# Two expert layers: 64 of 256 tokens look their experts up, 192 go through all experts; plain float32 first weights, ten products a unit

## The reference, cut to what matters

```python
def block(xc):                                   # per 128 tokens
    q = (xc @ w_q).reshape(128, 8, 2, 128)
    sc = einsum('thpd,hpnd->thpn', q, subkeys)   # 2 x 128 keys a head
    s1, i1 = top_k(sc[:, :, 0], 16)
    s2, i2 = top_k(sc[:, :, 1], 16)
    cand = s1[..., :, None] + s2[..., None, :]   # 256 sums a head
    top, pos = top_k(cand, 16)
    idx = ...i1 * 128 + i2 at pos...             # [128 tokens, 128 experts]
    gate = softmax(top)
    u_e, v_e = u[idx], v[idx]                    # u, v: [16384, 1024]
    act = gelu(einsum('ted,td->te', u_e, xc))
    return einsum('te,ted->td', gate * act, v_e)
```

## Time and profile before

| | |
|---|---|
| median of three runs | 2287.76 us (2285.74 to 2288.77) |
| profiled execution, first to last instruction | 2284.1 us |
| PE busy | 2268.4 us, 99% |
| DVE busy | 1699.0 us, 74% |
| ACT busy | 1324.8 us, 58% |
| POOL busy | 430.5 us, 19% |
| moved by DMA | 408.53 MB, 179 GB/s on average |
| PE's share of the chain that ended last | 87% |

### The profile page before, as it was taken

The page is one execution under the profiler, slowest core; times in us unless marked ns, Lnnn a source line. Parts: engine busy times, 40 slices in busy tenths (PEclk is TensorE's granted clock), DMA queues, the critical chain, the costliest instruction groups (busy, mean ns, idle before and its releaser), DMA issues.

```text
span 2284.1 us, 33324 instructions
## 1 busy us (share of the span) xinstructions
PE 2268.4 (99%) x12380; PEld 1929.4 (84%) x12380; DVE 1699.0 (74%) x3098; ACT 1324.8 (58%) x2181; POOL 430.5 (19%) x355
## 2 busy tenths in 40 slices
PE   9999999999999999999999999999999999999999
PEld 9788888888888888887788888888888888877887
DVE  7567588999975555668758898997555666877885
ACT  3454555578765554646555558776555564666554
POOL 1000233178710000000013316872000000000000
PEclk9999999999999999999999999999999999999999
DMA  7455455544455655644455554445556575333555
GB/s 257 156 176 190 161 191 189 183 167 156 149 194 193 203 193 194 231 163 142 141 171 187 193 177 169 153 155 190 194 193 232 184 227 179 135 123 118 185 186 173
DMA packets 112096, 408.53 MB, mean 179 GB/s; under 512 B 12592, under 2 KB 12640, under 8 KB 111680
## 3 DMA queue, kind: packets, MB, share of 16 engines
q1 hardware_dynamic: 107712, 391.63, 50.4%
q0 software_dynamic: 3504, 13.47, 1.7%
q10 hardware_dynamic: 720, 1.31, 0.2%
HBM read 405.30 MB, written 1.05 MB: 178 GB/s over the span
## 4 chain that ended last, share of the span: by engine, by line
PE 87%; DVE 9%; ACT 2%; issue 1%; DMA 1%; POOL 0%; ACTq 0%; DVEq 0%
PE ps L716 24%; PE ps L633 21%; PE ps L705 12%; PE ps L636 11%; PE ps L672 3%; PE ps L669 3%; PE ps L676 3%; DVE lo L1967 3%; PE ps L915 2%; PE ps L768 1%; DVE big L1973 1%; ACT hi L1373 1%; DVE big L2303 1%; PE ps L889 1%; PE ps L616 1%
## 5 line engine op out<-in xcount | busy, mean ns | idle before, releaser
L1967 DVE TENSOR_TENSOR lo<-raw,hi 128x1024 fp32r<-128x1024 f32 (+1 forms) x627 | 765.4, 1224 | 366.1 <-ACT hi L1373 363.6
L1373 ACT ACTIVATE hi<-raw 128x1024 fp32r<-128x1024 f32 x677 | 714.3, 1057 | 479.7 <-PE ps L716 270.7
L633 PE MATMUL ps<-xs,hi 128*128 128x512 f32 x2560 | 650.8, 396 | 1.0 <-DVE big L2918 1.0
L633 PEld LDWEIGHTS ps<-xs,hi 128*128 128x128 f32 x2560 | 459.2, 189 | 83.6 <-DVE big L2918 1.1
L636 PEld LDWEIGHTS ps<-xs,lo 128*128 128x128 f32 x2560 | 349.0, 190 | 25.8
L636 PE MATMUL ps<-xs,lo 128*128 128x256 f32 x2560 | 356.3, 282 | 0.0
L2998 POOL TENSOR_SCALAR lnp<-iota,selT 128x128 f32<-128x128 f32 x256 | 278.1, 1097 | 167.0 <-DVE negT L2345 88.9
L705 PE MATMUL ps<-hi,lefts 128*128 128x512 f32 x986 | 304.0, 389 | 0.0
L716 PE MATMUL ps<-lo,lefts 128*128 128x512 f32 x986 | 303.7, 389 | 0.0
L716 PE MATMUL ps<-hi,lefts 128*128 128x512 f32 x986 | 303.6, 389 | 0.0
L716 PEld LDWEIGHTS ps<-hi,lefts 128*128 128x128 f32 x986 | 184.9, 188 | 38.7 <-DVE lefts L2033 0.2
(11 more groups left out here) (370 smaller groups left out, 2505.8 us busy)
## 6 DMA issues: line engine op xcount, KB each, us to landing
raw<-in_peer_u SPq DMA_DIRECT2D x256, 512.0 KB, 3.2
raw<-in_peer_v SPq DMA_DIRECT2D x256, 512.0 KB, 4.2
raw<-in_ret_vg SPq DMA_DIRECT2D x32, 512.0 KB, 3.2
raw<-in_peer_q SPq DMA_DIRECT2D x24, 512.0 KB, 3.2
raw<-in_ffn_up SPq DMA_DIRECT2D x22, 512.0 KB, 3.3
raw<-in_ffn_down SPq DMA_DIRECT2D x22, 512.0 KB, 4.0
raw<-in_ffn_gate SPq DMA_DIRECT2D x18, 512.0 KB, 4.3
raw<-in_ret_qk SPq DMA_DIRECT2D x16, 512.0 KB, 4.6
```

The costliest lines, as they stand in the source:

```text
L633: e.matmul(out, uh[:, k, :], xs[:, k, :, :].rearrange("p h t -> p (h t)"), start=k == 0, stop=False)
L1373: e.activation(parts(i)[0][:, 0:w], raw[:, i % N_RAW, 0:w], ACT.Copy).then_inc(s_hi, 1)
L1967: e.tensor_tensor(ul[:, 0:w], raw[:, i % N_RAW, 0:w], uh[:, 0:w].bitcast(F32), ALU.subtract).then_inc(s_lo, 1)
```

## The change

**64 tokens are looked up.** The first 64 tokens (of token tile 0) use gathers: for each layer, 64 gathers of u rows and 64 of v rows. Each gather brings 128 rows of 4 KB, one to a partition: partitions 0 to 63 hold one chosen expert of each token, partitions 64 to 127 another. DVE multiplies a u gather with copies of x and sums it (`look`, q < 64), and later adds a v gather times its weight to `Peer.sums`. POOL issues the gathers from its queue (`look_up`), with four row buffers.

**192 tokens stay dense.** The first weights are no longer split: `peer_u` leaves the ring of units, and SP loads it into `plain` (six places over the room of `hi` and `lo`). PE multiplies 8 slices of plain float32 weights with 192 columns of plain float32 x (`Peer.xT`). The groups of four tokens are 48 instead of 64.

**Ten products a unit.** For tile 0 of the second weights the left side is one block of 128 columns: the low parts of its 64 dense tokens in columns 0 to 63 and their high parts in 64 to 127. It is multiplied with the high and the low weights (4 products of 512 columns, `mixed`); tile 1 keeps its 6. At the end `fold` adds the two halves and the looked-up sums with four plain float32 products.

**Moved.** The top-16 steps run 15 a unit and must be done in chunk 12; PE turns the gates at c == 14 (was 34). The 50 group steps stand in c >= 17, five in every nine units (were in c >= 36, five in every four). Looks stand three in every five units from c == 9, then five in every nine units of `peer_v`. POOL's low parts move from 25 units of `peer_u` to every third of the first 99 units of `peer_v`. The diff, cut to its core:

```diff
-FREE = 84
+LOOKED = 64
+DENSE = S - LOOKED
+GROUPS = DENSE // 4
+N_PLAIN, N_ROWS = 6, 4
+YIELDS, LISTED, SPREAD, LOOKS = 15, 14, 17, 9
+LOOK_PAIRS = 64
...
+            n = 1 if c >= SPREAD and (2 * (c - SPREAD) + j) % 9 < 5 else 0
+            steps[c, j] = list(range(at, min(at + n, GROUPS + 2)))
...
+            n = 1 if c >= LOOKS and (2 * (c - LOOKS) + j) % 5 < 3 and q < LOOK_PAIRS else 0
+            looks[c, j] = list(range(q, q + n))
...
+    for k in range(128):
+        n = 1 if k >= 3 and q < 2 * LOOK_PAIRS and (k - 3) % 9 < 5 else 0
+        looks[k] = list(range(q, q + n))
...
-        POOL_UNITS = (*range(1, 27, 2), *range(35, 59, 2))
+        POOL_UNITS = tuple(range(3, 99, 3))
...
+            for r in range(N_SPLIT):
+                n = min(n for n in in_ring[r] if n >= end)
+                m = max(m for m in range(128 * l, 128 * l + 128) if m % N_PLAIN % N_SPLIT == r)
+                W.after[n] = (*W.after.get(n, ()), (s_pused, m + 1))
@@ PE, first weights @@
-                        feat_wide(n + j, u.view[:, j, :], X_PEER[l])
+                        e.wait_ge(*plain_landed(m))
+                        for k in range(8):
+                            ins = e.matmul(u.view[:, j * DENSE:(j + 1) * DENSE], w[:, k, :], Peer.xT[:, k, :],
+                                           start=k == 0, stop=k == 7)
...
-                    if c == 34:
+                    if c == LISTED:
                         for t in range(2):
                             e.wait_ge(s_gate, 2 * l + t + 1)
@@ PE, second weights @@
+                def mixed(k):
+                    (uh, ul), left = parts(n0 + k), left_parts(q0 + k)[0][:, 0:128]
+                    e.wait_ge(s_hi, n0 + k + 1)
+                    e.wait_ge(s_ll, q0 + k + 1)
+                    for i, w in enumerate((uh, ul)):
+                        if i:
+                            e.wait_ge(*low(n0 + k))
+                        for f in range(2):
+                            ins = e.matmul(us[f].view, left, w[:, f * 512:(f + 1) * 512], start=k == 0 and i == 0,
+                                           stop=k == 127 and i == 1)
...
+            def fold(l):
+                e.wait_ge(*looked(l, 2 * LOOK_PAIRS))
...
+                for f in range(2):
...
+                    e.matmul(y.view, Peer.fold[:, LOOKED:192], Peer.sums[:, cut], start=True, stop=False)
+                    e.wait_ge(*use["mixed", l, f].freed)
+                    e.matmul(y.view, Peer.fold[:, 0:128], Peer.halves[:, cut], start=False, stop=True).then_inc(y.filled[0], 1)
-            peer(0, 0, between=lambda j: xs_tile(X_DIFF, xk, normed_x(1), 0) if j == 4 else None)
+            peer(0, 0, between=lambda j: xs_tile(X_DIFF, xk, normed_x(1), 0) if j == 5 else None)
@@ DVE, left side of the second weights @@
+                    if src.shape[-1] == DENSE:
+                        e.tensor_tensor(left_h[:, 0:128 - n], src[:, 0:128 - n], left_h[:, n:128].bitcast(F32), ALU.subtract)
+                        e.tensor_tensor(left_l[:, 128:S], src[:, 128 - n:DENSE], left_h[:, 128:S].bitcast(F32),
+                                        ALU.subtract).then_inc(s_ll, 1)
@@ DVE, beside the norm: two calls @@
+                def plain_xT(t):
...
+                    for g in range(2):
...
+                        e.tensor_copy(Peer.xT[:, 4 * g:4 * g + 4, mine], v[:, :, there]).then_inc(s_xt, 1)
...
+                def look(q):
...
+                    e.wait_ge(*rows_landed(l, q))
+                    if q < LOOK_PAIRS:
+                        e.tensor_tensor_reduce(rows, rows, Peer.copies, 1.0, 0.0, ALU.mult, ALU.add,
+                                               Peer.act[:, q:q + 1]).then_inc(s_looked, 1)
+                    else:
...
+                        e.scalar_tensor_tensor(out=Peer.sums, in0=rows, scalar=w, in1=Peer.sums, op0=ALU.mult,
+                                               op1=ALU.add).then_inc(s_looked, 1)
...
-                        if c < 33 and (c, j) != (0, 0):
-                            for _ in range(5 + (j and c % 2)):
+                        if c < LISTED - 1 and (c, j) != (0, 0):
+                            for _ in range(YIELDS):
                                 next(steps, None)
...
                 def last(k):
                     if k == 0:
-                        add(63)
...
+                        gated(63)
+                    for q in LOOKS_AT[k]:
+                        look(q)
@@ POOL @@
+            def look_up(l, q):
+                table = A[f"peer_ur{l}"] if q < LOOK_PAIRS else A[f"peer_v{l}"].rearrange("n p d -> (n p) d")
+                m, i = 2 * LOOK_PAIRS * l + q, q % LOOK_PAIRS
+                if q >= N_ROWS:
+                    e.wait_ge(*looked(l, q - N_ROWS + 1))
+                e.indirect_dma_start(out=Peer.rows[m % N_ROWS], out_offset=None, in_=table,
+                                     in_offset=bass.IndirectOffsetOnAxis(ap=Peer.idx[:, i:i + 1], axis=0)
+                                     ).then_inc(s_row[m % N_ROWS], 16)
...
+                copies(l)
+                list_out(l)
...
+                for q in range(N_ROWS + 2):
+                    look_up(l, q)
+                gates_out(l)
...
+                for i in range(GROUPS):
+                    while q < GATHERS[i]:
+                        look_up(l, q)
+                        q += 1
                     build(l, i)
...
+                for k in range(128):
+                    if k in POOL_UNITS:
+                        low_part(W.first[f"peer_v{l}"] + k)
+                    for q2 in LOOKS_AT[max(0, k - 2)]:
+                        if q2 + N_ROWS < 2 * LOOK_PAIRS:
+                            look_up(l, q2 + N_ROWS)
```

More of the change, by code:

```diff
@@ L571, in build @@
                 if i >= N_SPLIT:
-                    place(W.first[stage] + k, Tail.w[i - N_SPLIT], *read(stage, 95))
+                    i -= N_SPLIT
+                    place(W.first[stage] + k, Tail.w[i], *read(stage, -(-(Tail.w_at[i] + 2 * UNIT) // DENSE)))
             for i in range(6):
-                L.own[lhs_first[stage] + 122 + i] = (*Tail.left[i], read(stage, 95))
-        place(W.first["diff_k0"] + 3, Tail.more[0], *read("peer_v0", 103))
-        for i in range(3):
-            place(W.first["diff_q0"] + i, Tail.more[1 + i], *read("peer_v0", 128))
+                L.own[lhs_first[stage] + 122 + i] = (*Tail.left[i], read(stage, 115))
+        place(W.first["diff_k0"] + 3, Tail.first[0], looked(0, 2 * LOOK_PAIRS))
+        for i in range(2):
+            place(W.first["diff_q0"] + i, Tail.first[1 + i], looked(0, 2 * LOOK_PAIRS))
+        place(W.first["diff_q0"] + 2, Tail.first[3], *read("peer_v0", 126))
         for i in range(4):
@@ L581, in build @@
             place(W.first["diff_w_out"] + 6 + i, Diff.late[i], (s_scored, 16))
-        place(W.first["w_in_c"] + 3, Tail.more[0], *read("peer_v1", 128))
+        place(W.first["w_in_c"] + 3, Tail.more[0], *read("peer_v1", 128), (s_norm, 13))
         for i in range(3):
@@ L2259, in topk @@
                                     ALU.subtract).then_inc(s_sel, 1)
+                    if t == 0:
+                        first, second = (a.rearrange("p h k -> p (h k)") for a in Peer.sel[0][0:2])
+                        e.scalar_tensor_tensor(out=Peer.listed, in0=first, scalar=128.0, in1=second, op0=ALU.mult,
+                                               op1=ALU.add).then_inc(s_idx, 1)
                     yield
@@ new lines, in copies, with list_out @@
+            def copies(l):
+                e.wait_ge(s_norm, 8 * l + 4)
+                for s in range(2):
+                    e.dma_start(Peer.copies[64 * s:64 * s + 64, :], x[0:LOOKED, 0, :]).then_inc(s_xrep, 16)
+            def list_out(l):
+                e.wait_ge(s_idx, l + 1)
+                for s in range(2):
+                    e.dma_start(Peer.idx[64 * s:64 * s + 64, :], Peer.listed[0:LOOKED, 64 * s:64 * s + 64]).then_inc(s_list, 16)
+                e.memset(Peer.sums, 0.0).then_inc(s_zero, 1)
+                e.wait_ge(s_list, 32 * (l + 1))
@@ new lines, in gates_out, with make_fold @@
+            def gates_out(l):
+                e.wait_ge(s_gate, 2 * l + 1)
+                gate = Peer.sel[0][2].rearrange("p h k -> p (h k)")
+                for s in range(2):
+                    e.dma_start(Peer.gate[64 * s:64 * s + 64, :], gate[0:LOOKED, 64 * s:64 * s + 64]).then_inc(s_lgate, 16)
+            def make_fold(l):
+                e.wait_ge(s_oha, GROUPS * (l + 1))
+                e.wait_ge(s_ohv, GROUPS * (l + 1))
+                me.did(e.memset(Peer.fold, 0.0))
+                me.wait()
+                e.tensor_tensor(Peer.fold[:, LOOKED:128], ident[:, 0:64], ident[:, 64:128], ALU.add).then_inc(s_fold, 1)
@@ L3071, in sp, with plain_load @@
                     e.wait_ge(*low(n - N_RAW))
+                src = W.src[n]
                 e.dma_start(raw[:, n % N_RAW, 0:src.shape[-1]], src).then_inc(s_raw[n % N_RAW], 16)
+            def plain_load(l, i):
```

(19 more changed lines are left out.)

295 lines of the change are left out of this document (198 added, 97 removed).

## The result

The changed kernel takes 2349.7 us, the median of four runs (2344.9 to 2357.4), against 2287.3 us before in the same session: a ratio of 1.0275, 95% interval 1.0254 to 1.0296. It is slower. The forecast was 2309 us (+21), range 2225 to 2382; +62 was measured. In the profiled executions the spans are 2284.1 and 2345.3 us, 61.2 us apart, and I account for these.

The account below looks back on a forecast made before the run. PE, 87% of the chain, was taken as the bound before the change. Per layer, +3.5 us outside the second weights' pace and +6.9 from it, times two layers, gave +21 on 2287.8: 2309 us, range 2225 to 2382.

Parts of the forecast that it names:

- The unit of first weights: First weights: eight plain products of 192 columns take 2.62 us a unit, not 2.79, saving 22 us a layer.
- the gate wait of 22: First weights: PE waits 22 us a layer for DVE's top-16 steps and gates, bounds 16 to 26.
- the transition of 3.8: From first to second weights: PE waits 3.8 us a layer for unit 0's low part.
- The restart of 3: After the gates: POOL must issue look-ups before its first build, charged 3 us a layer (0 to 6).
- Two limits near 2.8 us that wait for each other: Second weights, units 3 to 98: DVE and POOL excluding each other, and the raw places' round; 2.88 us a unit.
- 18 x 2.6 behind unit 98: Second weights after unit 98: DVE makes all low parts, 2.43 us a unit, taken as 2.6 for 18 units.
- 11 x 2.27 at the end: Second weights, last 11 units: each takes 2.27 us, the time of PE's ten products.
- Layer 2 taken as layer 1: Whole sum: both layers priced alike, 3.5 + 6.9 us each, +21 us in all.
- The transfers alone: Rival, second weights: transfers alone limit the pace, 2.68 us a unit on average, 2273 us; chance 0.18.
- Look-ups hold POOL: Rival, second weights: POOL's low part stands behind gathers waiting for DVE, 390 us a stage, 2379 us; chance 0.13.
- PE sets the pace: Rival, second weights: ten products at 2.27 us a unit set the pace, 2180 us; chance 0.14.
- The fear about the clock: After a 22 us wait PE's clock might fall to 1.2 GHz, a few units each 2.62 us dearer.

Follow-up runs that it names:

- b4: The changed kernel with the gates turned on PE after unit pair 24 and the first group after pair 27: 2317.9 us.
- a1: The changed kernel with VectorE making all low parts of the second weights and GpSimd none: 2305.2 us.
- b1: The changed kernel with seven places for raw second weights, not three (units 2 to 118 of layer 1, 2 to 86 of layer 2): 2303.0 us.
- c3: The changed kernel with all low parts on VectorE, gates after pair 24, seven raw places (layer 2: five after unit 86): 2183.0 us.
- b2: The changed kernel with all low parts on VectorE and seven raw places (layer 1 to unit 118, layer 2 to 86): 2231.8 us.

## Why the prediction was too low

The direction was right, the measured time lies inside the range, and the two limits are there. The size was not: +62 us and not +21. The term that failed is the length of the second weights, which the forecast had at 355 us a layer, 363 with what it put at their two ends (3.8 and 4.5 us). They took 382.5 and 386.0 us. Point by point:

- *The unit of first weights*, 2.62 us: 2.60 measured. Right. Sixteen groups fewer (a spread takes 0.52 us, forecast 0.53), the gate wait of 22 (20.9), the transition of 3.8 (3.8): right. The restart of 3 did not come (0.2): PE, slowed by the clock, came for the first group just when POOL had it ready. In b4 it was 5.1.
- *Two limits near 2.8 us that wait for each other, 2.88 taken for units 3 to 98*: right in size, 2.87 and 2.91 in layer 1, and right in kind. Lifting one leaves about 2.7 (a1: 2.72 and 2.69; b1: 2.68 and 2.77), lifting both leaves 2.36, most of it PE's. Either alone was forecast at 2.67 to 2.82. For the ring this agreement is partly luck: 2.77 was worked out for the place of POOL's low parts, and in a1, where POOL makes none, the three places still hold the pace at 2.7.
- *18 x 2.6 behind unit 98*: failed. It measured 2.94 and 2.99, +6 and +7 us. I priced VectorE's load (2.43) and put a little on top. But short looks leave 2.93 / 2.88, seven raw places bring 2.36, and fewer looks and gathers 2.59: it is the round of the three raw places, with its landings beside gathers, that sets the pace there. I had worked this round out only for the place that POOL's low parts use.
- *11 x 2.27 at the end*: failed in layer 1. Units 117 to 127 came at 2.55 us and not at PE's pace, and the held-back halves (six of 1.36 us) and the fold then ran behind the last unit instead of in its gaps. From unit 117's left part, ten spacings ahead of the last at 1013.74, to the next stage at 1028.8 is 40.5 us against 25.0 for the eleven units and 4.5 for the fold: +11 us. In layer 2 it was +2. The places have a part in this (1.88 with seven of them, c3). The clock can have one: it stood at 0.50 for nearly 7 us just before unit 127, up to 3 us (estimate), and no run separates it:

```profile
1006.00:1013.00 7.00, 5.25 (x11) 3.44 (x12) 5.06 (x10) 4.18 (x7) 0.00 (x0) 0.51 0.77 231
```

- *Layer 2 taken as layer 1*: failed. Units 51 to 99 measured 3.15 there, +13 us. The second input's work on VectorE and ScalarE was covered before, when PE set the pace (350.1 us against 349.1), and is not any more. The same units in layer 1 and layer 2:

```profile
795.80:935.30 139.50, 118.01 (x480) 87.20 (x480) 120.70 (x158) 61.38 (x94) 82.16 (x47) 1.00 0.83 282
1746.10:1897.10 151.00, 124.16 (x496) 92.76 (x496) 126.89 (x199) 70.34 (x119) 88.45 (x54) 0.97 0.79 273
```

  VectorE has 6.2 us and ScalarE 9.0 us more to do, and the lower clock (0.97) can have cost up to 5 us (estimate). How the 13 us divide between these isn't shown. "What costs nothing because PE is the bound" has to be priced again once PE isn't.
- *The first plain load of layer 2* was priced at nothing: PE waits 4.4 us for it (L990's row above), nearly all of the 4.5 us by which +5.5 misses the forecast of +1.

Together in the second weights: 1 + 6 + 11 in layer 1 and 13 + 7 + 2 in layer 2, 40 us, against 39 (69.3 - 30.4) to be explained. These are lengths of stretches, read from the starts of the left parts; the clock's share is in them.

The rivals. *The transfers alone* (2.68 a unit): b2 ran units of the same bytes at 2.36, with 357 GB/s over 240 us. The 348 GB/s that I took from the earlier trace rows as the full rate was too low. *Look-ups hold POOL*: POOL waited for looks, but its low parts were not what PE waited for most (L2168 was). Its own price was a little high: 3.2 us up to unit 98 with the tail of the likeliest case make 386 us, not 390. *PE sets the pace*: false for this kernel, and true for most units of b2. The fear about the clock was too large for the gate waits, 1.9 us behind the first, and left out the rest: the sum has no term for a clock that falls in the second weights, behind waits far shorter than 22 us (none over 2.2 us between 700 and 900 us, where it fell once). The trace of before had a row for it that I missed. After a PE wait of 1.21 us at 1129 us the clock was down, though every slice of the page reads full:

```profile
1130.00:1134.00 4.00, 4.00 (x13) 2.99 (x13) 1.38 (x2) 1.52 (x3) 0.00 (x0) 0.57 0.59 245
```

## What to carry to other kernels

When two limits of a ring lie within a few per cent, take each away by itself and both together. One by one they gave 45 and 47 us here, together 118; the waits view of one run didn't tell which mattered, and even the sign "the high part waits for PE" stood in b1, where PE was idle for 11%. Before work goes to GpSimd to relieve VectorE, count what both read: beside two-input VectorE operations, a low part of 1.22 us on VectorE cost it 2.2 us when GpSimd made it. And when the bound leaves PE, go through everything in the stage, its end and its other layer again, that PE had covered.

## What the runs showed of the hardware

- GpSimd's gather instruction was longest where VectorE made all the low parts: a mean of 1885 ns in a1 and 2428 in b2, against 1384 in the changed kernel and 1485 in b1, where POOL made some (660 to 900 us, the same bytes). VectorE's busy share doesn't order them: it was 80% in a1 and 93% in b1. Why, no run shows. In a1 and b2:

```profile
L3188 POOL DMA_INDIRECT big<-in_peer_v,big x50 | 94.2, 1885 | 161.3 <-DVE big L2513 159.0 <-issue 2.3
```

```profile
L3218 POOL DMA_INDIRECT big<-in_peer_v,big x58 | 140.8, 2428 | 122.6 <-DVE big L2543 119.9 <-issue 2.6
```

- The core moved more than I had read from the earlier trace rows: 365 GB/s over 10 us in the windows above, and 415 in this one of the changed kernel:

```profile
610.00:620.00 10.00, 10.00 (x78) 9.80 (x77) 5.38 (x11) 2.87 (x10) 5.95 (x6) 1.00 1.02 415
```

  The Trainium skill ("DMA: Bandwidth & Descriptors", Where 436 GB/s comes from) gives about 358 GB/s as the HBM side's limit for a core, half of what it gives for the two cores of a stack; here one core works, this row stands above it, and the measurement decides.
- Landings of a raw unit in the second weights, min/median/max: before, and in b2 with seven places and the gathers beside them. With more loads in flight and the gathers beside them a load lands later, and the pace is higher all the same:

```profile
DMA to landing us min/median/max: 3.1/4.3/6.3
```

```profile
DMA to landing us min/median/max: 3.8/5.4/9.6
```
